# The last softmax head taken second half first, and three groups of its output projection begun in banks of their own

## The reference, cut to what matters

```
# 8 heads, 128 + 64 (rotary) features for q and k, 128 for v, blocks of 128 queries
s = (einsum('bqhd,bkhd->bhqk', qn, k_nope) + einsum('bqhr,bkr->bhqk', qr, k_rope)) * scale
s = where(key_pos <= q_pos, s, -inf)
p = softmax(s, axis=-1)
y = einsum('bhqk,bkhv->bqhv', p, v)                       # all blocks, all heads
y_mla = y.reshape(B, S, 8 * 128) @ w_mla_o
mixed = (sigmoid(gate_a) * y_gla + sigmoid(gate_b) * y_mla) @ w_out
h = LN(alpha * h + mixed)
```

## Time and profile before

| | |
|---|---|
| median of 3 runs | 1812.95 us |
| profiled execution | 1811.56 us |
| its span | 1809.8 us |
| mean granted TensorE clock | 0.993 |
| busy: PE, DVE, ACT, POOL | 97%, 56%, 41%, 45% |
| last head and its aftermath in the trace | some 929 to 988 us |

### The profile page before, as it was taken

One profiled execution on the slowest core, in us unless ns is written; L12 is line 12 of the kernel. 1 busy time (PEld: TensorE's weight loads), 2 busy tenths in 40 slices (PEclk: granted clock), 3 DMA queues, 4 the chain that ended last, 5 costly groups with the idle time before them and its releaser, 6 DMA issues.

```text
span 1809.8 us, 23398 instructions
## 1 busy us (share of the span) xinstructions
PE 1756.7 (97%) x8464; PEld 1460.2 (81%) x8464; DVE 1021.8 (56%) x1763; ACT 751.1 (41%) x1396; POOL 813.4 (45%) x668
## 2 busy tenths in 40 slices
PE   8999999999999999999988999999999999999997
PEld 6788887888888777788877888778888888778886
DVE  6313312534444467454544635477777776688799
ACT  6534433243344214454553103564444444444442
POOL 6888654221212353333332356687777777400000
PEclk9999999999999999999999999999999999999999
DMA  5433324214122278422332452434334442585333
GB/s 169 137 105 122 111 90 152 59 49 92 47 101 86 99 247 279 127 79 83 111 123 93 156 194 70 163 113 143 111 111 149 150 149 94 203 289 188 95 97 117
DMA packets 216975, 233.29 MB, mean 129 GB/s; under 512 B 24157, under 2 KB 147213, under 8 KB 216861
## 3 DMA queue, kind: packets, MB, share of 16 engines
q1 hardware_dynamic: 181246, 167.57, 29.5%
q10 hardware_dynamic: 35616, 64.24, 10.0%
HBM read 160.19 MB, written 71.58 MB: 128 GB/s over the span
## 4 chain that ended last, share of the span: by engine, by line
PE 77%; DVE 10%; DMA 3%; POOL 3%; ACT 3%; issue 2%; SPq 1%; ACTq 0%; DVEq 0%; POOLq 0%
PE psum_all L1167 22%; PE psum_all L1169 22%; PE psum_all L1168 21%; PE psum_all L1504 1%; PE psum_all L1488 1%; PE psum_all L1505 1%; PE psum_all L1506 1%; DVE pT_lo L1691 1%; DMA ga_st<-d_sga 1%; PE psum_all L1231 1%; PE psum_all L1235 1%; PE psum_all L1233 1%; DVE w_lo L1691 1%; DMA fa_raw<-d_f 1%; PE psum_all L1202 1%
## 5 line engine op out<-in xcount | busy, mean ns | idle before, releaser
L1045 POOL CAST w_hi<-w_raw 128x512 fp32r<-128x512 f32 (+3 forms) x82 | 67.8, 826 | 345.3 <-PE psum_all L1169 336.9
L1167 PE MATMUL psum_all<-xT_hi,w_hi 128*128 128x512 f32 (+1 forms) x456 | 182.2, 399 | 5.3 <-POOL w_lo L981 3.3
L1168 PE MATMUL psum_all<-xT_lo,w_hi 128*128 128x512 f32 (+1 forms) x456 | 179.1, 393 | 0.0
L1169 PE MATMUL psum_all<-xT_hi,w_lo 128*128 128x512 f32 (+1 forms) x456 | 179.0, 393 | 0.0
L1047 POOL TENSOR_TENSOR w_lo<-w_raw,w_hi 128x512 fp32r<-128x512 f32 (+3 forms) x82 | 144.6, 1764 | 6.7
L1167 PE MATMUL psum_all<-t_hi,w_hi 128*128 128x512 f32 x352 | 137.9, 392 | 3.3 <-DVE psum_all L2305 2.7
L1168 PE MATMUL psum_all<-t_lo,w_hi 128*128 128x512 f32 x352 | 137.7, 391 | 0.0
L1169 PE MATMUL psum_all<-t_hi,w_lo 128*128 128x512 f32 x352 | 137.5, 391 | 0.0
L1107 POOL TENSOR_TENSOR w_lo<-w_raw,w_hi 128x512 fp32r<-128x512 f32 x88 | 115.7, 1322 | 37.9 <-ACT w_hi L2994 37.8
L1061 POOL TENSOR_SCALAR p_sb<-p_sb,small 128x128 f32<-128x128 f32 (+3 forms) x64 | 48.1, 751 | 171.6 <-DVE small L2069 171.5
L1107 POOL TENSOR_TENSOR w_lo<-s_sb,w_hi 128x512 fp32r<-128x512 f32 x66 | 86.3, 1309 | 61.0 <-ACT w_hi L2994 61.0
(11 more groups left out here) (548 smaller groups left out, 5023.6 us busy)
## 6 DMA issues: line engine op xcount, KB each, us to landing
w_raw<-in_w_up_dram SPq DMA_DIRECT2D x44, 512.0 KB, 4.9
fa_raw<-d_f SPq DMA_DIRECT2D x76, 256.0 KB, 2.6
w_raw<-in_w_in_dram SPq DMA_DIRECT2D x36, 512.0 KB, 4.6
d_f<-up_g SPq DMA_DIRECT2D x44, 256.0 KB, 3.0
d_f<-f_sum SPq DMA_DIRECT2D x33, 256.0 KB, 2.6
w_raw<-in_w_out_dram SPq DMA_DIRECT2D x8, 1024.0 KB, 5.0
wd<-in_w_down_dram SPq DMA_DIRECT2D x22, 256.0 KB, 6.6
x_tok<-in_x_dram SPq DMA_DIRECT2D x8, 512.0 KB, 6.7
```

Source lines behind the costliest of these rows:

```text
L1045: wc.done(nc.gpsimd.tensor_copy(w_hi[b][:, w], src[:, w]))
L1167: pe.matmul(out_ap, ah, bh, start=start and i == 0, stop=False, skip_group_check=more)
L1168: pe.matmul(out_ap, ah, bl, start=False, stop=False, skip_group_check=more)
L1169: last = pe.matmul(out_ap, al, bh, start=False, stop=stop and i == len(terms) - 1, skip_group_check=more)
```

## The change

The last head (h = 7) takes its blocks in the order 4, 5, 6, 7, 0, 1, 2, 3 (`block_at`). Its second token half is thus complete in step 59, its first in step 63. Whatever depended on a block's number (widths, the count of transpose groups in `tgroup`, columns) follows `block_at`.

Group g of the projection now has the second token half where g is even (`mo_half`), so the groups 2 and 0 that come first read the second half. K tile 7 is two tiles of half the width, `mT7[1]` for the second half and `mT7[0]` for the first. The second is cast and split in step 62 (in `EARLY`), the first behind the loop.

Groups 2, 0 and 1 are begun in banks 3, 7 and 1 and stay there until they are complete: `mo_part`, its two copies on ACT, its two additions on DVE and their semaphores are gone, and the groups in the projection take turns over five banks (3, 7, 1, 0, 2). `MO_FILL` lists single pairs of group and K tile from step 57 on. Tiles 1 to 4 are loaded one step earlier, tiles 0 to 4 are cast and split one step earlier, tile 6 is loaded in step 60 and split in step 61 as before, and tile 5 is loaded in step 61 and split in step 64 (the old `OM_LOAD` holds places in the list `early`, the new one tile numbers). In step 65 the transposes of step 63 come ahead of the fill. `wout` waits for 16 instead of 15 low parts at its second part.

```diff
+        mT7 = [[put(f"mT7{half}{p}", (P, HALF), kb + 2 * i, F32R, home) for i, p in enumerate("hl")]
+               for half, kb, home in ((0, 56, A0), (1, 56, R0))]
+        def block_at(s):
+            h, i = divmod(s, TT)
+            return h, (i + 4) % TT if h == MH - 1 else i
-        EARLY = {55: 0, 56: 1, 57: 2, 58: 3, 59: 4, 61: 6, 64: 5}
-        OM_LOAD = {53: 0, 55: 1, 56: 2, 57: 3, 58: 4, 60: 5, 61: 6}
+        EARLY = {54: 0, 55: 1, 56: 2, 57: 3, 58: 4, 61: 6, 62: 7, 64: 5}
+        OM_LOAD = {53: 0, 54: 1, 55: 2, 56: 3, 57: 4, 60: 6, 61: 5}
         early = list(EARLY.values())
+        loads = list(OM_LOAD.values())
         MO_ORDER = (2, 0, 1) + tuple(range(3, 16))
-        MO_FILL = {59: (0, (0, 1)), 60: (0, (2, 3)), 61: (0, (4,)), 62: (1, (0, 1, 2)), 63: (1, (3, 4)), 64: (2, (0, 1, 2)), 65: (2, (3, 4, 6))}
+        def mo_half(g):
+            return slice(0, HALF) if g % 2 else slice(HALF, S)
+        MO_FILL = {57: ((0, 0), (0, 1)), 59: ((0, 2),), 60: ((0, 3), (1, 0)), 61: ((1, 1), (1, 2)), 62: ((0, 4), (1, 3)),
+                   63: ((1, 4), (2, 0)), 64: ((2, 1), (2, 2), (2, 3)), 65: ((2, 4), (0, 6), (1, 6), (2, 6)), 66: ((0, 5), (2, 5))}
...
         def mo_bank(g):
-            return psum[g % 4] if g else psum[7]
+            return psum[(3, 7, 1, 0, 2)[g % 5]]
...
-                if s in MO_FILL:
-                    g, ks = MO_FILL[s]
-                    pe.wait_ge(sm["ad2"], early.index(ks[-1]) + 1)
-                    if ks[0] == 0 and g:
-                        pe.wait_ge(sm["mo_part"], g)
-                    last = split3(psum[7], mo_terms(g, ks), start=ks[0] == 0, stop=ks[-1] == 4 and g < 2)
-                    if ks[-1] == 4 and g < 2:
-                        last.then_inc(sm["mo_fill"], 1)
+                if s == STEPS + 1:
+                    probs_t(s - 2)
+                mo_fill(s)
                 if s >= 3 and (s - 3) % 4 == 3:
                     values(s - 3)
-                if 2 <= s < STEPS + 2:
+                if 2 <= s < STEPS + 1:
                     probs_t(s - 2)
             for i, g in enumerate(MO_ORDER):
-                if i == 0:
-                    pe.wait_ge(sm["ad2"], KT)
-                    split3(psum[7], mo_terms(g, [5, 7]), start=False).then_inc(sm["mo_mm"], 1)
-                    continue
                 if g == 1:
+                    split3(mo_bank(i), mo_terms(g, [5]), start=False, stop=False, more=True)
                     pe.wait_ge(sm["ad2"], KT + 1)
                 if i >= 5:
                     pe.wait_ge(sm["mo_ev"], i - 3)
-                split3(mo_bank(i), mo_terms(g, [6, 5, 7] if g < 2 else early + [7])).then_inc(sm["mo_mm"], 1)
+                ks = [KT - 1] if g < 3 else [0, 1, 2, 3, 4, 6, 5, 7]
+                split3(mo_bank(i), mo_terms(g, ks), start=g >= 3, more=g < 3).then_inc(sm["mo_mm"], 1)
...
-                    pe.wait_ge(sm["mix_lo"], 15 if part else 8)
+                    pe.wait_ge(sm["mix_lo"], 16 if part else 8)
...
-            ve.wait_ge(sm["vd2"], KT)
-            split_lo(mT[7][1][:, 0:HALF], om_st[0][:, :], mT[7][0][:, 0:HALF]).then_inc(sm["ad2"], 1)
             ve.wait_ge(sm["vd2"], KT + 1)
-            split_lo(mT[7][1][:, HALF:S], psum[6], mT[7][0][:, HALF:S]).then_inc(sm["ad2"], 1)
+            split_lo(mT7[0][1][:, :], psum[6], mT7[0][0][:, :]).then_inc(sm["ad2"], 1)
...
-                if s in (61, 63):
-                    ac.wait_ge(sm["mo_fill"], (s - 59) // 2)
-                    A.copy(mo_part[(s - 61) // 2][:, :], psum[7]).then_inc(sm["mo_part"], 1)
```

More of the change, by code:

```diff
@@ L231, in block_kernel @@
         MT_AT = (0, 1, 2, 5, 4, 3, 6, 7)
-        mT = [[put(f"mT{k}{p}", (P, S), 8 * MT_AT[k] + 4 * i, F32R, A0) for i, p in enumerate("hl")] for k in range(KT)]
+        mT = [[put(f"mT{k}{p}", (P, S), 8 * MT_AT[k] + 4 * i, F32R, A0) for i, p in enumerate("hl")] for k in range(KT - 1)]
+        mT7 = [[put(f"mT7{half}{p}", (P, HALF), kb + 2 * i, F32R, home) for i, p in enumerate("hl")]
+               for half, kb, home in ((0, 56, A0), (1, 56, R0))]
         r = Region(R0, RSZ)
@@ L235, in block_kernel @@
         r = Region(R0 + 64 * KB, RSZ - 64 * KB)
-        mo_part = [nc.alloc_sbuf_tensor_at(f"mo_part{i}", [P, HALF], F32, offset=R0 + (56 + 2 * i) * KB) for i in range(2)]
         sgb_st = [r(f"sgb_st{i}", [P, HALF]) for i in range(2)]
@@ L521, in block_kernel @@
                  "hT_mm up_mm fs_hi fs_lo dn_mm dn_ev ln2_v ln2_s ln2_ok ad2 vd2 "
-                 "mo_part mo_fill f_sums s_ok up_hi up_w snap u_sum t_pool g_id g_c g_si v_id v_c f_ok t_dve t_act h_stored par_mm par_ok out_stored ").split()
+                 "f_sums s_ok up_hi up_w snap u_sum t_pool g_id g_c g_si v_id v_c f_ok t_dve t_act h_stored par_mm par_ok out_stored ").split()
         sm = {n: sem(n) for n in names}
@@ L541, in block_kernel @@
         f_out = [sem("f_out0"), sem("f_out1")]
+        def block_at(s):
+            h, i = divmod(s, TT)
+            return h, (i + 4) % TT if h == MH - 1 else i
         def tgroup(s, g=0):
-            h, qb = divmod(s, TT)
+            h, qb = block_at(s)
+            if h == MH - 1:
+                return 12 * h + (2 * (qb - 4) if qb >= 4 else 8 + qb) + g
             return 12 * h + (qb if qb < 4 else 4 + 2 * (qb - 4)) + g
@@ L1510, in mo_terms, with mo_fill @@
                 n = need(("mlao", g // 4))
-                hs = slice(g % 2 * HALF, (g % 2 + 1) * HALF)
-                return [(w_part(n, k, g % 4 // 2 * P, P), w_part(n, k, g % 4 // 2 * P, P, True), mT[k][0][:, hs], mT[k][1][:, hs]) for k in ks]
+                hs = mo_half(g)
+                parts = [[t[:, :] for t in mT7[(g + 1) % 2]] if k == KT - 1 else [t[:, hs] for t in mT[k]] for k in ks]
+                return [(w_part(n, k, g % 4 // 2 * P, P), w_part(n, k, g % 4 // 2 * P, P, True), *part) for k, part in zip(ks, parts)]
+            def mo_fill(s):
+                for g, k in MO_FILL.get(s, ()):
+                    pe.wait_ge(sm["ad2"], early.index(k) + 1)
+                    split3(mo_bank(MO_ORDER.index(g)), mo_terms(g, [k]), start=k == 0, stop=False, more=True)
             pe.wait_ge(*ev_at[gid[("p0", 3)]])
@@ L2083, in _ @@
                     k = EARLY[s]
-                    m = early.index(k)
-                    ve.wait_ge(sm["vd2"], m + 1)
-                    split_lo(mT[k][1][:, :], ld2[m % 2][:, :], mT[k][0][:, :]).then_inc(sm["ad2"], 1)
-            ve.wait_ge(sm["vd2"], KT)
-            split_lo(mT[7][1][:, 0:HALF], om_st[0][:, :], mT[7][0][:, 0:HALF]).then_inc(sm["ad2"], 1)
+                    ve.wait_ge(sm["vd2"], early.index(k) + 1)
+                    if k == KT - 1:
+                        split_lo(mT7[1][1][:, :], om_st[0][:, :], mT7[1][0][:, :]).then_inc(sm["ad2"], 1)
+                    else:
+                        split_lo(mT[k][1][:, :], ld2[loads.index(k) % 2][:, :], mT[k][0][:, :]).then_inc(sm["ad2"], 1)
             ve.wait_ge(sm["vd2"], KT + 1)
-            split_lo(mT[7][1][:, HALF:S], psum[6], mT[7][0][:, HALF:S]).then_inc(sm["ad2"], 1)
+            split_lo(mT7[0][1][:, :], psum[6], mT7[0][0][:, :]).then_inc(sm["ad2"], 1)
             for i in range(17):
@@ L2098, in _ @@
                         ve.wait_ge(sm["mix_lo"], i - 1)
-                    if g < 2:
-                        V.tensor_tensor(mx[i % 2][:, :], mo_bank(i), mo_part[g][:, :], ALU.add).then_inc(sm["mo_ev"], 1)
-                        ve.wait_ge(sm["mo_ev"], i + 1)
                     ve.wait_ge(mx_in[i % 2], 32 * (i // 2 + 1))
[L2103 to L2107, removed]
+                    V.tensor_tensor(mx[i % 2][:, :], mo_bank(i), sgb_st[i % 2][:, :], ALU.mult).then_inc(sm["mo_ev"], 1)
+                    ve.wait_ge(sm["mo_ev"], i + 1)
                     V.tensor_tensor(mx[i % 2][:, :], mx[i % 2][:, :], mm_st[i % 2][:, :], ALU.add).then_inc(sm["mix_ok"], 1)
@@ L2874, in om_load @@
             def om_load(m):
-                k = early[m]
+                k = loads[m]
                 ac.wait_ge(om_out[0], 16 * (k + 1))
@@ L2938, in _ @@
                     probs_out(s)
-                if s in (61, 63):
-                    ac.wait_ge(sm["mo_fill"], (s - 59) // 2)
-                    A.copy(mo_part[(s - 61) // 2][:, :], psum[7]).then_inc(sm["mo_part"], 1)
                 if s in OM_LOAD:
-                    m = OM_LOAD[s]
+                    m = loads.index(OM_LOAD[s])
                     if m >= 2:
-                        ac.wait_ge(sm["ad2"], m - 1)
+                        ac.wait_ge(sm["ad2"], early.index(loads[m - 2]) + 1)
                     om_load(m)
@@ L2948, in _ @@
                     k = EARLY[s]
-                    m = early.index(k)
+                    if k == KT - 1:
+                        A.copy(mT7[1][0][:, :], om_st[0][:, :]).then_inc(sm["vd2"], 1)
+                        continue
+                    m = loads.index(k)
                     if k == 5:
@@ L2953, in _ @@
                     A.copy(mT[k][0][:, :], ld2[m % 2][:, :]).then_inc(sm["vd2"], 1)
```

(7 more changed lines are left out.)

28 lines of the change are left out of this document (14 added, 14 removed).

## The result

The changed kernel takes 1800.86 us (median of 4 runs, 1799.95 to 1803.74) against 1812.64 us for the kernel before, measured beside it: ratio 0.994, 95% interval 0.9927 to 0.9953. Forecast was 1803.0. The profiled execution took 1800.69 us with a span of 1799.0 us, 10.8 less than before.

A forecast was written before the change was run, and what follows sets the result against it. PE, busy 97% of the span, bounds the kernel. Losses of 13.4 us before against 3.45 us of stalls now leave 9.95, taken as 10.0: 1812.95 - 10.0 = 1803.0 us, range 1799.5 to 1807.5.

The forecast's parts named there:

- Where the kernel loses: From step 56's scores to the first whole projection group: 13.4 us lost before; stretch 48 to 49 us after, from 58.7.
- the steps: PE starts laid out step by step in the new order: group 3 starts at 977.95 instead of 988.23, 10.3 us less.
- the sum: Losses before, 13.4 us, against remaining stalls of 3.45 us, counted from start to start: 9.95 us gained.
- The remaining stalls: PE waits in steps 56, 57, 58 and 60: 1.5, 0.4, 1.2 and 0.35 us, 3.45 in all.
- Bank 7 and half clock: Fill of step 64: the 2.36 us wait for bank 7 to be emptied and the half clock behind it, 1.5, both go.
- The values of 63: Value product of step 63: two K tiles of fill in step 66 come before it, so its 1.56 us stall goes.
- The thin margin: Transposes of step 63 in step 64: the division is ready at 968.5, a margin of 0.25 us, the thinnest.
- The end of the loop: Behind the values of 63: 2.05 us of matmuls cover 1.7 of bank 6's cast and low part, 0.3 to 0.5 spare.
- the 1.44 goes: PE's 1.44 us stall for mT7 at the end of the loop was to disappear.
- SBUF contention in the early steps: DVE's splits beside POOL's divisions: charged nothing; a collision costs at most 1.1 us in each of five steps.
- The mix: Its first eviction, at 987.63 before, comes at about 982; group 5 starts at 988.9, with 6 us of room.
- C's low end: Clock rival, one fewer half-clock stretch and the remaining stalls hidden as well: 1798.9 us; chance 0.09.

The follow-up runs named there:

- the second profile: The changed kernel run and profiled once more with no edit: 1802.34 us, ratio 0.9946 to the kernel before.
- one bank: Changed kernel with its new block order, but groups 0, 1 and 2 one after the other in bank 7 with mo_part: 1807.42 us, ratio 0.9967.
- the fill first: Changed kernel with the transposes of step 63 behind the fill of step 65 again: 1802.67 us, ratio 0.9932.
- the kernel before with early splits: Kernel before, tiles 0 to 4 loaded and split one step earlier, two K tiles filled in step 57: 1812.96 us, ratio 0.9998.
- late splits: Changed kernel with loads and splits of tiles 0 to 4 one step later, fill of step 57 moved to 59: 1802.51 us, ratio 0.9944.
- low parts last: Changed kernel, tile 0 split first, other tiles' low parts behind maximum, reciprocal and probabilities' low parts, K tile 1 filled in step 59: 1800.18 us, ratio 0.9939.

## Why the prediction was right

- **Where the kernel loses.** Right. The stretch fell by 58.72 - 47.71 = 11.0, forecast 10.3 by the steps and 9.95 by the sum. Worked out from the starts of all PE instructions in both traces, the 11.0 are 8.7 of stalls (11.9 before, 3.2 now, each 0.16 longer than shown), 1.6 of half clock (put at 1.5) and 0.7 of slightly longer gaps between instructions, which the sum had left out. That, with the stalls put 0.3 too high, is why 47.71 lies just under the 48 to 49 that were named.
- **The remaining stalls.** Forecast 1.5, 0.4, 1.2 and 0.35 in starts. Measured, with 0.16 for each modelled end, 1.35, 0.41, 1.02 and 0.38, at the same four places; in the second profile the second is 0.77.
- **Bank 7 and half clock.** Right in the mechanism: with one bank the wait returned, 1.66 and 0.84, and the stretch grew by 3.9 to 4.3, against 2 to 4 expected. The half clock did not return with it, and other stalls of 0.57 and 0.26 came in its place. The stall of 2.36 and the half clock appear in both variants of the kernel before that keep its fill of step 64.
- **The values of 63.** Right in the result. The thin margin that I named at the transposes of 63 held (the division of 63 ends at 966.18; they follow three transposes that start at 966.02, so they start at about 966.3). The run with the fill first shows that their new order did not remove the old 1.56. What did was not run alone. In the trace the low parts of 63 end at 969.83, the fill of step 66 starts at 969.53 and the values at 970.89; without that fill PE would have waited 0.3 (an estimate from these rows), so most of the 1.56 went with the shorter block and what lies before it.
- **The end of the loop.** mT70l ends at 974.26 (973.57 and 0.69), PE takes it at 974.85: 0.6 to spare, forecast 0.3 to 0.5. But the early split of tile 7 is worth more than the term "the 1.44 goes". Without it the changed kernel loses 5.8 to 6.1, not 1.44. POOL's instruction is released by tile 5's split and the low part behind the loop, over ACT's cast, by the values of 63. Before, these lay 6.5 us apart (974.69 to 981.2), and POOL was through at 981.32 when the low part came at 981.87. In the new order, with the short value product last and no stall before it, they lie 3.7 apart (968.97 to 972.7), and the low part comes 2.2 before POOL ends. I had the SBUF contention in the text and looked for it only in the early steps.
- **SBUF contention in the early steps.** Charged at nothing, rightly: divisions of 1.01, 1.12 and 0.80. Tile 1's cast starts at 930.86, when the division of step 54 has just ended (930.85). The price is shown by the variants: 0.9 for each division (put at 1.1), 2.07 for a low part.
- **The mix.** Its first eviction is at 977.04, forecast about 982; the loads that it waits for came 4.1 us behind the values of 63 and not 6.4 as before. Nothing waits for it.
- **The time.** 1803.0 was forecast by subtracting 10.0 from 1812.95. The two sets of runs give 11.8 and 10.05 less; the excess of the first is within what runs move. One side sum was wrong: C's low end. Its 3.45 already counts the stalls from start to start, so the 4 x 0.16 are in it twice, and the fewer half clock that the sentence starts from is missing; 1803.0 - 1.5 - 3.45 gives 1798.1 and not 1798.9. The range and the forecast do not hang on it.

By part, the 10.6 to 11.0 us come from the block order with its half tile and the later tile 5 (5.4), the banks (3.9 to 4.3) and the early splits with the fill of 57 (0.6 to 1.4, by the kernel that they are put into). The first of these was not taken apart: what the block order does without the half tile and the fill of step 66 is not shown.

## What to carry to other kernels

When the last phase of a pipeline runs dry, try to reorder it so that its long blocks lie beside the extra work and its short ones at the end: the short ones need one bank where the long ones need two, and the freed banks let partial sums stay where they are. Price a step that becomes earlier also by what it would meet in its old place after the change, since everything released by the faster engine moves up too. Put a DVE instruction with two SBUF inputs where POOL has nothing to do, or give it a PSUM input.

## What the runs showed of the hardware

- A DVE subtraction of 512 columns with two SBUF inputs took 2.76 us when it came during a POOL instruction of 4.54, and 0.69 without one; with one PSUM input it took 0.69 inside a POOL instruction of 4.61, and 0.68 without one. It goes both ways: POOL's division took 1.90 for 1.01 where DVE's low part started with it. This is the exclusive lock of the Trainium skill ("SBUF — State Buffer", "Who interferes with whom"). These runs agree with it in who is stretched and which operands matter.
- The length of a PE stall did not by itself tell whether half clock follows. Stalls of 1.66, 2.23 and 2.34 us (the last in the kernel before with early splits) had none behind them, 2.36 had a period of 3.4 us in three kernels, and 3.51 one of 6.8 us.
- One and the same wait later in the kernel, at about 1149 to 1152 us, was followed by 6.8 us at half clock in the first profile of the changed kernel (stall 2.83), by 3.4 in the second (2.75), and by none in the runs with late splits (2.51) and with low parts last (3.00, granted clock 1.00 from 1148 to 1160). The first profile has 1.9 us more behind the stretch than the kernel before, and 2.4 more than the second.
